# Two bias rows of a hybrid attention and gating layer: spread over the partitions by TensorE instead of loaded as equal rows

## The chip, the cores and the metric

The kernel runs on the 8 cores of one Trainium2 chip. Each core computes one of the 8 batch entries; the cores exchange nothing. The time of a run is the device time of the slowest core, in microseconds (us). Three runs of the kernel before took 498.07, 499.13 and 499.91 us; their median is 499.13 us.

## The reference, cut to what matters

For each batch entry, x is 4096 x 1024 in f32. The layer computes

```python
h = rmsnorm(x, norm_g)
proj = h @ w_in + b_in                      # 1024 -> 2816 columns
q, k, v, z_a, u_s, v_s, z_s = split(proj)   # 512,128,128,512,512,512,512
attn = banded_sink_attention(q, k, v, sinks) * silu(z_a)      # window 128, 8 heads of 64, 2 kv heads
u_s, v_s = gelu(u_s), gelu(v_s)
sgu = u_s * (W_s @ layernorm(v_s) + b_s) * silu(z_s)          # per chunk of 128 positions
out = rmsnorm(x + concat(attn, sgu) @ w_out + b_out, final_norm_g)
```

The change is about two slices of `b_in`: the 128 values added to `v` and the 512 values added to `v_s`, the gating input.

## The kernel before

**Tiling.** Each core walks 8 sections (`st`) of 512 positions, each of four tiles of 128 positions. In a section, the tiles of x are squared and summed, scaled by the reciprocal root (`square_x`, `rstd_x`, `scale_x`) and transposed to `xT` (`transpose_x`: by TensorE on an identity in sections 0 and 1, by DMA later). TensorE then multiplies by `w_all`, the bf16 input weights in 22 column blocks of 128 (`cb` 0 to 21: u 0-3, v_s 4-7, z_s 8-11, z_a 12-15, q 16-19, k 20, v 21). Most column blocks come out with channels on the partitions, where the bias is one value per partition and is read from `bias_fm`, columns 8 to 29 of the small constant `pack_a`. Two come out with positions on the partitions, so their bias varies along the free axis and has to stand in every partition: v (L637, reads `bv_bc`) and v_s (L668, reads `bvs`). Before, `bvs` is loaded from `bvs_bc`, 128 equal rows of 512 f32 (256 KB), and `bv_bc` is a slice of `pack_b`, 128 equal rows of 128 f32 (64 KB of the 198 KB).

**The opening.** x tiles 0 to 3 are issued first on the SP queue, `pack_a` on ACT's queue, then the 22 weight blocks of 512 KB each (`load_w`, L510-522). A weight block lands in one of 8 staging buffers (four in `xe`, four in `mixT`) and is scaled by `norm_g` and cast into `w_all` by DVE or POOL (L521); the load of block cb + 8 waits for that cast. In between stand the small constants, placed by `SMALL_AFTER` (L41): `bvs` behind block 2, `pb` behind 14, the gating weights and `bsB` behind 21. The four x tiles of section 1 are issued among blocks 14 to 18 (L38). TensorE runs 27 idle matmuls on zeros (L1000, `stir`) at the start and 4 more after each of the first three tiles' transposes; then u (`by_tile`, L575), v_s (`vs_first`, L647), and the other blocks (L588) as their weights come.

**What sets the order.** The program is a list of operations with estimated costs (`cost`, us) and priorities (`prio`). A planner (`Scheduler`) places them at build time, engine by engine, at the earliest estimated start, ties by priority; the result is a fixed instruction order on each engine with semaphore waits. Operations with a priority above -0.5 (`OPENING`) get a random shift from `SEEDS`, one seed per section, drawn by the operation's number in the list (L152-155). PSUM banks are handed out by the planner too: class "P" may hold 4 of the 8 at a time.

```python
    load_const(key, dst, src, eng="sp", kb=kb, prio=-1.4 + 0.01 * cb + 0.005, after=[w_op[cb]])   # L968
    o.prio += by if o.prio > OPENING and o.dsem is None else 0.0                                # L155
```

Of the kernel before, what the change touches and what calls it, by code (L numbers as in the profile page):

```python
# [8 lines left out]
F32 = mybir.dt.float32  # L9
# [15 lines left out]


PA_G, PA_BIAS, PA_ID, PA_W = 0, 8, 30, 94
PB_SINK, PB_LNB, PB_LNG, PB_BV, PB_MK, PB_MC, PB_W = 0, 4, 8, 12, 140, 332, 396


MIX0 = 5
# [6 lines left out]
X1_AFTER = (15, 16, 17, 18)  # L38
W_OUT_AFTER = 20
W_OUT_BEHIND = (2, 3, 3, 3, 3, 3, 3, 3)  # L40
SMALL_AFTER = {"bvs": 2, "pb": 14, "wT": 21, "bsB": 21}  # L41

STIR = (27, 4)
OPENING = -0.5
# [15 lines left out]
LAST_PARTS = (512, 384, 128)  # L60
LAST_APART = {NT - 4: "act", NT - 3: "dve", NT - 2: "dve"}

SEEDS = (49966, 300, 14147, 300, 300, 300, 300, 70794)
JITTER = 0.04


# [321 lines left out]
def build_program():  # L388
    nc = bass.Bass("TRN2", target_bir_lowering=False)

    def din(name, shape, dt=F32):
        return nc.dram_tensor(name, list(shape), dt, kind="ExternalInput").ap()
# [3 lines left out]
    wout_d = din("w_out", [D, D])  # L396
    pa_d = din("pack_a", [128, PA_W])
    pb_d = din("pack_b", [128, PB_W])
    bvs_d = din("bvs_bc", [128, 512])
    wT_d = din("sgu_wT", [128, 8, 128])  # L400
    bsB_d = din("bsB", [128, 4, 128])
    bout_d = din("bout_bc", [128, D])
# [3 lines left out]
    with ExitStack() as es:  # L406
        def sb(name, shape, dt):
            return es.enter_context(nc.sbuf_tensor(name, list(shape), dt))
# [21 lines left out]
        mixT = sb("mixT", [128, 2, 8, 512], BF16)  # L430
        sgt = sb("sgt", [128, 2, 512], F32)
        junk = sb("junk", [128, D], BF16)
        ones64 = sb("ones64", [128, 64], BF16)
        esink = sb("esink", [128, 4], F32)
        bvs = sb("bvs_sb", [128, 512], F32)
        WT = sb("WT_bf", [128, 8, 128], BF16)
# [4 lines left out]
        bias_fm = pa[:, PA_BIAS:PA_BIAS + NCB]  # L441
        ident = pa[:, PA_ID:PA_W].bitcast(BF16)
        lnb, lng = pb[:, PB_LNB:PB_LNB + 4], pb[:, PB_LNG:PB_LNG + 4]
        bv_bc = pb[:, PB_BV:PB_BV + 128]
        mask6, mask_c = pb[:, PB_MK:PB_MC].bitcast(BF16), pb[:, PB_MC:PB_W].bitcast(BF16)
        bout = sb("bout_sb", [128, D], F32)
        gf = sb("gf_sb", [128, D], F32)
# [15 lines left out]
        def bank(h):  # L463
            return pp[:, h.at, :]
# [155 lines left out]
        def qkv(st):  # L620
            qb, ks = st % 2, (st % 3) * 4
            v0 = st - 1.0
            for c in range(4):
                fm_group(st, CB_Q + c, qT[:, qb, c, :], ("qT", qb, c), None, v0 + 0.02 + 0.06 * c)
            fm_group(st, CB_K, kT[:, ks:ks + 4, :].rearrange("p a b -> p (a b)"), ("kT", st % 3), None, v0 + 0.26)
            h = Bank("P")
            xb = st % 2

            def mmv(e):
                for tt in range(4):  # L630
                    for k in range(8):
                        ins = e.matmul(bank(h)[:, tt * 128:(tt + 1) * 128], lhsT=xT[:, xb, k, tt * 128:(tt + 1) * 128],  # L632
                                       rhs=w_all[:, CB_V, k, :], start=(k == 0 and tt == 0), stop=(k == 7),
                                       skip_group_check=True)
                return ins
            G.op("pe", mmv, reads=[("xT", xb, t) for t in range(4)] + [("w", CB_V)], cost=1.79, alloc=[h], prio=v0 + 0.3, mode="full")
            G.op("dve", lambda e: e.tensor_tensor(out=v_r[:, ks:ks + 4, :], in0=bank(h).rearrange("p (a c) -> p a c", a=4),  # L637
                                                  in1=bv_bc.unsqueeze(1).to_broadcast([128, 4, 128]), op=ALU.add),
                 uses=[h], reads=["c_bv"], writes=[("v", st % 3)], cost=0.68, prio=v0 + 0.3)

        def vs_first(hs):
# [147 lines left out]
        def attention(st, j):  # L789
# [9 lines left out]
            def mmpv(e):  # L799
                def half(qh, what, g):  # L800
                    return pp[g * 64:(g + 1) * 64, hv.at + qh, what * 256:(what + 1) * 256]

                def weights(what, slot, r, g):
                    return ones64[r, :] if what else v_r[r, slot, g * 64:(g + 1) * 64]

                for what in range(1 if n else 2):
                    for kh, slot in ((0, cur), (1, prev)) if n else ((0, cur),):
                        r = slice(kh * 64, (kh + 1) * 64)
                        for g in range(2):
                            e.matmul(half(kh, what, g), lhsT=weights(what, slot, r, g), rhs=PT[r, p2, blk(BLK_Z[g])], start=what == 0,  # L810
                                     stop=False, skip_group_check=True)
                for what in range(2):
                    for qh, where, slot in ((1, BLK_X, cur), (0, BLK_Y, prev)) if n else ((1, BLK_X, cur),):
                        for g in range(2):
                            ins = e.matmul(half(qh, what, g), lhsT=weights(what, slot, slice(0, 128), g), rhs=(ET if what and n else PT)[:, p2, blk(where[g])],  # L815
                                           start=n == 0 and what == 0, stop=True, skip_group_check=True)
                return ins
# [127 lines left out]
        def finish_end(n, y, key, v0, parts):  # L945
# [15 lines left out]
            hold[NT - 2].after += (last_add[-1],)  # L961
            hold[NT - 3].after += (last_add[0],)

        def setup_late():
            stage_w = LR[:].rearrange("p a (h t) -> p (a h) t", t=128)
            def small(key, dst, src, name, kb):
                cb = SMALL_AFTER[name]
                load_const(key, dst, src, eng="sp", kb=kb, prio=-1.4 + 0.01 * cb + 0.005, after=[w_op[cb]])  # L968

            small("c_bvs", bvs[:], bvs_d, "bvs", 256)  # L970
            small(["c_sink", "c_lnb", "c_lng", "c_bv", "c_mask"], pb[:], pb_d, "pb", 198)
            small([("LR", 0), ("LR", 1)], stage_w, wT_d, "wT", 512)
            small("c_bsB", Cmat[:], bsB_d, "bsB", 256)
            G.op("dve", lambda e: e.tensor_tensor(out=WT[:], in0=stage_w, in1=mask_c.unsqueeze(1).to_broadcast([128, 8, 128]), op=ALU.mult),
                 reads=[("LR", 0), ("LR", 1), "c_mask"], writes=["WT"], cost=1.2, prio=-0.3, port=True)
            G.op("act", lambda e: e.activation(out=esink[:], in_=pb[:, PB_SINK:PB_SINK + 4], func=AF.Exp), reads=["c_sink"], writes=["esink"], cost=0.25,
                 prio=0, phase=PH_EXP)
            h = Bank("P")

            def cmat_mm(e):  # L980
                for jj in range(4):
                    for hh in range(2):
                        ins = e.matmul(bank(h)[hh * 64:(hh + 1) * 64, jj * 128:(jj + 1) * 128], lhsT=ones64[:, :], rhs=WT[:, 2 * jj + hh, :],
                                       start=(jj == 0), stop=True, skip_group_check=True)
                return ins
            G.op("pe", cmat_mm, reads=["ones64", "WT"], alloc=[h], cost=0.6, prio=-0.3, mode="col")

            def cm(e):
                for jj in range(4):
                    ins = e.scalar_tensor_tensor(out=Cmat[:, jj, :], in0=bank(h)[:, jj * 128:(jj + 1) * 128], scalar=lnb[:, jj:jj + 1],  # L990
                                                 in1=Cmat[:, jj, :], op0=ALU.mult, op1=ALU.add)
                return ins
            G.op("dve", cm, uses=[h], reads=["c_lnb"], writes=["c_bsB"] + [("Cmat", jj) for jj in range(4)], cost=1.3, prio=-0.3)
            load_const("c_bout", bout[:], bout_d, eng="sp", kb=512, prio=-0.3, after=[w_op[21]], reads=[("w_out", BOUT_AFTER)])
            load_const("c_gf", gf[:], gf_d, eng="sp", kb=512, prio=-0.3, after=[w_op[21]], reads=[("w_out", 7)])

        def stir(alloc, uses, count, after):
            def mm(e):
                for _ in range(count):
                    ins = e.matmul(bank(idle), lhsT=zsT[:, 0, 0:128], rhs=zsT[:, 0, :], start=True, stop=True)  # L1000
                return ins
            G.op("pe", mm, reads=[("zsT", 0)], alloc=alloc, uses=uses, cost=0.22 * count + (0 if uses else 4.0), prio=-9, mode="full", after=after)
# [15 lines left out]
        for tt in range(4):  # L1018
            square_x(0, tt)
            rstd_x(0, [tt])  # L1020
            scale_x(0, tt)
            o = transpose_x(0, tt)
            if tt < 3:
                stir((), [idle], STIR[1], [o])
        setup_late()
        gelu_part(0)
        silu_part(0)
# [39 lines left out]
def _host_layout(inp):  # L1067
# [10 lines left out]
    shared = {  # L1078
        "w_in": w_p,
        "w_out": w_out[rows, :],  # L1080
        "bvs_bc": np.broadcast_to(b_p[CB_VS:CB_VS + 4].reshape(1, 512), (128, 512)),
        "sgu_wT": np.asarray(inp["sgu_w"])[0].transpose(2, 0, 1),
        "bsB": np.repeat(np.asarray(inp["sgu_b"])[0].reshape(4, 2, 1, 128), 64, axis=2).reshape(4, 128, 128).transpose(1, 0, 2),
        "bout_bc": np.broadcast_to(np.asarray(inp["b_out"])[0], (128, D)),
# [3 lines left out]
    def words(m):  # L1088
        return np.ascontiguousarray(m.astype(ml_dtypes.bfloat16)).view(f32)
# [5 lines left out]
    lnb = np.asarray(inp["sgu_ln_b"])[0].reshape(4, 128).T  # L1095
    lng = np.asarray(inp["sgu_ln_g"])[0].reshape(4, 128).T
    shared["pack_a"] = np.concatenate([np.asarray(inp["norm_g"])[0].reshape(8, 128).T, b_p.T, words(eye)], axis=1)
    shared["pack_b"] = np.concatenate([sinks, lnb, lng, np.broadcast_to(b_p[CB_V], (128, 128)), words(mask6), words(mC)], axis=1)
    return {k: np.ascontiguousarray(v, dtype=f32) for k, v in shared.items()}


# [17 lines left out]
```

How the kernel before makes its waits and increments, by code:

```python
    def run(engine, items):  # L369
        for fn, waits, inc in items:
            for sem, val in waits:
                engine.wait_ge(sem, val)
            fn(engine).then_inc(inc[0], inc[1])
# [1 line left out]
    def sync(e):  # L375
        run(e, progs["sp"])
        for sem, val in finals.values():
            e.wait_ge(sem, val)
```

## Time and profile before

| what | value |
|---|---|
| three runs, median | 499.13 us (498.07 to 499.91) |
| profiled execution, its own time | 501.85 us |
| its span on the slowest core (core 5) | 500.3 us |
| spans of the eight cores | 495.9 to 500.3 us |
| busy on core 5 | PE 97%, DVE 71%, ACT 64%, POOL 36% |
| moved | 71.17 MB in the span, mean 142 GB/s |

The profiled execution took 501.85 us, 1.55 us more than the longest span of a core, and 2.72 us more than the median of the three runs. PE is TensorE's matmul row, PEld its weight loads, SPq the SP queue that issues transfers. An entry such as `L588` is a line of the kernel before. "Idle before" is the time an engine stood still just ahead of an instruction, and what ended it.

### The profile page before, as it was taken

The page shows a single profiled execution, that of the slowest core. Times are in us where ns is not written, and L with a number is a line of the kernel's source. Part 1 is how long each engine was busy: PE and PEld are TensorE (multiplying, and loading weights), DVE is VectorE, ACT ScalarE, POOL GpSimd, SP SyncE. Part 2 cuts the span into 40 slices and gives each one's busy share as a digit, 9 for nine tenths or more (in the row PEclk, how much of TensorE's full clock was granted, in tenths as well). Part 3 has the DMA queues.
Part 4 walks back from the last instruction along what each step waited for, and adds up shares of the span by engine and source line. Part 5 has one row for each costly group of instructions (what it writes and reads, how often), then busy time and mean ns, then how long its engine had stood idle before and what let it go on. Part 6 is the DMA issues. An engine that isn't in the chain of part 4 may idle for free.

```text
span 500.3 us, 10242 instructions; the slowest of 8 cores (495.9 to 500.3 us)
## 1 busy us (share of the span) xinstructions
PE 483.3 (97%) x3427; PEld 241.6 (48%) x3427; DVE 354.0 (71%) x537; ACT 319.8 (64%) x558; POOL 181.5 (36%) x223
## 2 busy tenths in 40 slices
PE   7797999999999999999999999999999999999994
PEld 3673455444544455444554445444554445444442
DVE  1678877596689448984696477773898547776795
ACT  3525665775688465965768565875659564567855
POOL 1114425444405121250245104470146733444144
PEclk9999899999999999999999999999999999999999
DMA  7999699488117911337413833355224422130035
GB/s 205 320 316 326 203 156 254 180 189 274 44 44 190 231 43 45 126 59 196 168 64 107 191 105 128 127 120 176 86 106 147 84 85 76 54 126 1 4 125 210
DMA packets 44116, 71.17 MB, mean 142 GB/s; under 512 B 27552, under 2 KB 27680, under 8 KB 44064
## 3 DMA queue, kind: packets, MB, share of 16 engines
q1 hardware_dynamic: 42768, 68.37, 44.9%
q0 software_dynamic: 1152, 2.10, 3.0%
q8 instruction: 28, 0.46, 0.4%
q14 instruction: 24, 0.20, 0.1%
q10 hardware_dynamic: 144, 0.05, 0.1%
HBM read 49.53 MB, written 16.78 MB: 133 GB/s over the span
## 4 chain that ended last, share of the span: by engine, by line
PE 82%; DMA 8%; DVE 4%; ACT 2%; issue 2%; SPq 0%; POOL 0%; DVEq 0%; ACTq 0%; POOLq 0%
PE pp L588 43%; PE pp L878 19%; PE pp L663 9%; DMA xe<-w_in 8%; PE pp L815 3%; PE pp L753 3%; PE pp L632 3%; PE pp L708 1%; PE pp L810 1%; DVE w_all L521 1%; ACT ET L771 1%; DVE ET L784 1%; ACT LR L835 0%; SPq L492 0%; DVE LR L841 0%
## 5 line engine op out<-in xcount | busy, mean ns | idle before, releaser
L588 PE MATMUL pp<-xT,w_all 128*128 128x512 bf16 x1056 | 237.0, 380 | 3.0 <-DVE w_all L521 2.7
L588 PEld LDWEIGHTS pp<-xT,w_all 128*128 128x128 bf16 x1056 | 101.6, 98 | 125.7 <-issue 7.2
L878 PE MATMUL pp<-w_out_bf,mixT 128*128 128x512 bf16 (+2 forms) x520 | 116.9, 376 | 0.4 <-DVE mixT L846 0.4
L869 POOL TENSOR_TENSOR xe<-xe,bout_sb 128x1024 f32<-128x1024 f32 x28 | 66.3, 2370 | 58.0 <-DMA xe<-x 20.6
L878 PEld LDWEIGHTS pp<-w_out_bf,mixT 128*128 128x128 bf16 x520 | 48.9, 98 | 58.3 <-issue 2.9
L771 ACT ACTIVATE ET<-pp 128x1536 bf16<-128x1536 f32 x32 | 46.4, 1451 | 12.4 <-PE pp L753 12.3
L663 PE MATMUL pp<-w_all,xT 128*128 128x512 bf16 x224 | 52.8, 384 | 0.6 <-DVE xe L885 0.3
L715 DVE SCALAR_TENSOR_TENSOR sgt<-pp,pack_b_sb,Cmat 128x512 f32<-128x512 f32 x32 | 23.7, 748 | 39.8 <-PE pp L708 39.1
L894 ACT ACTIVATE junk<-xe 128x1024 bf16<-128x1024 f32 x28 | 29.7, 1061 | 34.2 <-DVE xe L885 34.2
L899 POOL TENSOR_SCALAR st_fm<-st_fs 128x1 f32<-128x1 f32 x29 | 8.1, 281 | 111.6 <-ACT junk L894 110.9
L885 DVE TENSOR_TENSOR xe<-pp,xe 128x512 f32<-128x512 f32 x56 | 38.0, 685 | 8.6 <-PE pp L878 8.1
L835 ACT ACTIVATE LR<-pp,esink 128x128 f32<-128x128 f32 x128 | 36.4, 372 | 11.5 <-PE pp L815 7.6
L526 ACT ACTIVATE junk<-xa 128x1024 bf16<-128x1024 f32 x32 | 33.8, 1057 | 15.0 <-DMA xa<-x 14.3
L919 DVE SCALAR_TENSOR_TENSOR xe<-xe,st_fr,gf_sb 128x1024 f32<-128x1024 f32 x28 | 36.7, 1309 | 4.9 <-POOL st_fr L901 4.0
L670 ACT ACTIVATE vs_f<-vs_f 128x512 f32<-128x512 f32 x32 | 19.4, 625 | 27.0 <-DVE vs_f L668 23.8
L777 DVE TENSOR_TENSOR PT<-ET,pack_b_sb 128x1536 bf16<-128x1536 bf16 x32 | 32.3, 1010 | 5.6 <-ACT ET L771 4.9
L663 PEld LDWEIGHTS pp<-w_all,xT 128*128 128x128 bf16 x224 | 21.7, 99 | 27.6 <-issue 3.7
L616 ACT ACTIVATE zaT<-pp,pack_a_sb 128x512 bf16<-128x512 f32 x28 | 19.0, 686 | 23.7 <-PE pp L588 23.7
L485 ACT ACT_TABLE_LOAD x24 | 30.8, 1283 | 2.0 <-POOL ones L505 1.6
L784 DVE TENSOR_TENSOR ET<-PT 64x512 bf16<-64x512 bf16 x62 | 31.1, 503 | 1.3
L668 DVE TENSOR_TENSOR vs_f<-pp,bvs_sb 128x512 f32<-128x512 f32 x32 | 21.7, 685 | 13.2 <-PE pp L663 12.2
L841 DVE TENSOR_TENSOR LR<-LR,zaT 128x512 f32<-128x512 f32 x31 | 25.9, 834 | 6.7 <-ACT LR L839 6.5
(94 smaller groups left out, 583.2 us busy)
## 6 DMA issues: line engine op xcount, KB each, us to landing
xa<-x SPq DMA_DIRECT2D x32, 512.0 KB, 6.2
xe<-x SPq DMA_DIRECT2D x28, 512.0 KB, 3.4
out<-xe SPq DMA_DIRECT2D x28, 512.0 KB, 2.7
xe<-w_in SPq DMA_DIRECT2D x12, 512.0 KB, 14.0
mixT<-w_in SPq DMA_DIRECT2D x10, 512.0 KB, 15.6
w_out_bf<-w_out POOLq DMA_DIRECT2D x8, 256.0 KB, 11.9
out<-w_all SPq DMA_DIRECT2D x3, 512.0 KB, 2.7
LR<-sgu_wT SPq DMA_DIRECT2D x1, 512.0 KB, 20.7
```

What stands on the lines that cost most here:

```text
L485: return lambda e: e.activation(out=dmy[:, 1:2], in_=dmy[:, 0:1], func=func)
L526: G.op("act", lambda e: e.activation(out=junk[:], in_=xa[:, tt, :], func=AF.Square, accum_out=st_ss[:, par, tt:tt + 1]), reads=[("xa", tt) ...
L588: ins = e.matmul(bank(h), lhsT=w_all[:, cb, k, :], rhs=xT[:, xb, k, :], start=(k == 0), stop=(k == 7))
L663: ins = e.matmul(bank(h), lhsT=xT[:, xb, k, tt * 128:(tt + 1) * 128], rhs=w_all[:, CB_VS:CB_VS + 4, k, :], start=(k == 0), stop=(k == 7))
L771: G.op("act", lambda e: e.activation(out=ET[:, p2, :].rearrange("p (g b) -> p g b", g=2), in_=raw(), func=AF.Exp, scale=0.125), uses=[h], ...
L777: return e.tensor_tensor(out=v, in0=raw, in1=m, op=ALU.mult)
L784: return e.tensor_tensor(out=at[:, pick], in0=z[:, pick], in1=z[:, rest], op=ALU.add)
L835: ins = e.activation(out=LR[:, lb, c * 128:(c + 1) * 128].rearrange("p (h q) -> p h q", h=2), in_=banks_of(hv)[:, :, 256 + c * 64:256 + (c ...
L869: G.op("pool", lambda e: e.tensor_tensor(out=buf[:, s, :], in0=buf[:, s, :], in1=bout[:], op=ALU.add), reads=["c_bout"], writes=[key], cos ...
L878: ins = e.matmul(bank(h)[:, 0:width], lhsT=mixT[:, mb, ec, tt * 128:(tt + 1) * 128], rhs=w_out[:, ec, cols], start=(ec == 0), stop=(ec == 7))
L885: G.op("dve", lambda e, cols=cols, h=h, width=width: e.tensor_tensor(out=buf[:, s, cols], in0=bank(h)[:, 0:width], in1=buf[:, s, cols], op ...
L919: G.op("dve", lambda e: e.scalar_tensor_tensor(out=src, in0=src, scalar=st_fr[:, s:s + 1], in1=gf[:], op0=ALU.mult, op1=ALU.mult), reads=[ ...
```

## The change

The 256 KB transfer of `bvs_bc` is gone, and `pack_b` is 128 columns narrower (198 to 134 KB). In their place `spread_biases` makes the rows on the core. `bias_fm` (128 channels by 22 blocks, one value per partition) is split into three bf16 parts on DVE; each part's column is multiplied by the identity, which gives diagonal matrices; TensorE multiplies them by a 128 x 128 matrix of ones, which puts the sum of the three diagonals into every partition; ACT copies the two results from PSUM. `ones64` grows from 64 to 128 columns; its other users take the first 64. The diagonals lie in `ET`, which attention first uses much later. The list of operations is ten longer behind this point, and three of the eight seeds are others.

```diff
-PB_SINK, PB_LNB, PB_LNG, PB_BV, PB_MK, PB_MC, PB_W = 0, 4, 8, 12, 140, 332, 396
+PB_SINK, PB_LNB, PB_LNG, PB_MK, PB_MC, PB_W = 0, 4, 8, 12, 204, 268
-SMALL_AFTER = {"bvs": 2, "pb": 14, "wT": 21, "bsB": 21}
+SMALL_AFTER = {"pb": 14, "wT": 21, "bsB": 21}
-SEEDS = (49966, 300, 14147, 300, 300, 300, 300, 70794)
+SEEDS = (17612, 300, 30261, 300, 300, 300, 300, 61515)
...
-        ones64 = sb("ones64", [128, 64], BF16)
+        ones64 = sb("ones64", [128, 128], BF16)
...
-        bv_bc = pb[:, PB_BV:PB_BV + 128]
+        bv_bc = sb("bv_bc", [128, 128], F32)
+        b_part = sb("b_part", [128, 3, NCB], BF16)
+        b_left = sb("b_left", [128, NCB], F32)
...
+        def spread_biases():
+            parts = ET[:].rearrange("p a b -> p (a b)")[:, 0:1920]
+            d_vs = parts[:, 0:1536].rearrange("p (i c t) -> p i c t", i=3, c=4)
+            d_v = parts[:, 1536:1920].rearrange("p (i t) -> p i t", i=3)
+            for i in range(3):
+                left = b_left[:] if i else bias_fm
+                G.op("dve", lambda e, i=i, left=left: e.tensor_copy(out=b_part[:, i, :], in_=left), reads=["b_left"] if i else ["c_biasfm"],
+                     writes=[("b_part", i)], cost=0.1, prio=-8)
+                if i < 2:
+                    G.op("dve", lambda e, i=i, left=left: e.tensor_tensor(out=b_left[:], in0=left, in1=b_part[:, i, :], op=ALU.subtract),
+                         reads=["c_biasfm", ("b_part", i)], writes=["b_left"], cost=0.1, prio=-8)
+            at = [("b_part", i) for i in range(3)] + ["c_ident"]
+            G.op("dve", lambda e: e.tensor_tensor(out=d_vs, in0=ident.unsqueeze(1).unsqueeze(1).to_broadcast([128, 3, 4, 128]),
+                                                  in1=b_part[:, :, CB_VS:CB_VS + 4].unsqueeze(3).to_broadcast([128, 3, 4, 128]), op=ALU.mult),
+                 reads=at, writes=[("ET", 0), ("ET", 1)], cost=1.7, prio=-8)
+            G.op("dve", lambda e: e.tensor_tensor(out=d_v, in0=ident.unsqueeze(1).to_broadcast([128, 3, 128]),
+                                                  in1=b_part[:, :, CB_V:CB_V + 1].to_broadcast([128, 3, 128]), op=ALU.mult),
+                 reads=at, writes=[("ET", 0), ("ET", 1)], cost=0.5, prio=-8)
+            for key, d, dst, cost in (("c_bvs", d_vs, bvs, 0.66), ("c_bv", d_v, bv_bc, 0.17)):
+                h = Bank("P")
+                width = dst.shape[1]
+
+                def mm(e, h=h, d=d, width=width):
+                    for i in range(3):
+                        ins = e.matmul(bank(h)[:, 0:width], lhsT=ones64[:], rhs=d[:, i], start=(i == 0), stop=(i == 2))
+                    return ins
+                G.op("pe", mm, reads=["ones64", ("ET", 0), ("ET", 1)], alloc=[h], cost=cost, prio=-2.95, mode="full")
+                G.op("act", lambda e, h=h, dst=dst, width=width: e.activation(out=dst[:], in_=bank(h)[:, 0:width], func=AF.Copy), uses=[h],
+                     writes=[key], cost=0.2 + 0.45 * width / 512, prio=-1.9)
...
-            small("c_bvs", bvs[:], bvs_d, "bvs", 256)
-            small(["c_sink", "c_lnb", "c_lng", "c_bv", "c_mask"], pb[:], pb_d, "pb", 198)
+            small(["c_sink", "c_lnb", "c_lng", "c_mask"], pb[:], pb_d, "pb", 134)
...
+        spread_biases()
         setup_late()
```

## Rows read from the trace of the kernel before

**Rows 1.** The eight cores: span and mean granted clock.
```profile
core 0: 495.9 us, clock 0.996
core 3: 499.3 us, clock 0.996
core 4: 495.9 us, clock 0.997
core 5: 500.3 us, clock 0.995
```
**Rows 2.** Busy time by stretch (PE, PEld, DVE, ACT, POOL, clock, DMA): core 5, last core 3.
```profile
20.00:50.00 30.00, 27.52 (x306) 19.41 (x302) 23.13 (x31) 11.55 (x19) 7.98 (x12) 1.00 0.99 325
45.00:50.00 5.00, 2.52 (x17) 1.17 (x16) 3.92 (x8) 4.22 (x9) 1.03 (x3) 1.00 0.99 332
50.00:55.00 5.00, 4.73 (x15) 1.82 (x16) 3.94 (x8) 4.87 (x8) 1.65 (x3) 0.66 1.00 321
300.00:400.00 100.00, 100.00 (x664) 49.20 (x662) 72.95 (x112) 67.81 (x116) 45.14 (x50) 1.00 0.41 122
...
50.00:55.00 5.00, 5.00 (x30) 2.50 (x29) 4.68 (x7) 4.97 (x8) 2.23 (x4) 1.00 1.03 282
```
**Rows 3.** Core 5, chain that ended last, to 75 us: start, us, what.
```profile
31.32 17.38 DMA xe<-w_in
...
48.79 1.24 DVE w_all L521
50.02 0.24 issue
50.27 2.63 PE pp L588 x8
52.90 2.67 PE pp L663 x8
55.57 0.45 PE pp L559 x8
56.01 1.73 PE pp L588 x8
```
**Rows 4.** PE's waits to 75 us: core 5, core 3, core 0; total, times, longest.
```profile
PE pp L588 <- DVE w_all L521: 2.7, 2, 2.1
...
PE pp L588 <- DVE w_all L521: 2.5, 2, 1.5
...
PE pp L588 <- ACT zsT L616: 0.8, 1, 0.8
```
**Rows 5.** DMA issues of the whole span: KB each, median us to landing.
```profile
xe<-w_in SPq DMA_DIRECT2D x12, 512.0 KB, 14.0
bvs_sb<-bvs_bc SPq DMA_DIRECT2D x1, 256.0 KB, 13.8
...
out<-w_all SPq DMA_DIRECT2D x1, 256.0 KB, 2.5
...
pack_b_sb<-pack_b SPq DMA_DIRECT2D x1, 198.0 KB, 12.0
pack_a_sb<-pack_a ACTq DMA_DIRECT2D x1, 47.0 KB, 4.9
```
**Rows 6.** Core 5, timeline to 60 us: start, us, instruction, idle before.
```profile
1.06 0.40 ACTq L481 DMA_DIRECT2D pack_a_sb<-pack_a  x1
...
1.88 8.45 PE L1000 MATMUL pp<-zsT 128*128 128x512 bf16 x27 [1.88 <-DVE zsT L1016]
...
8.53 0.19 POOL L532 TENSOR_SCALAR st_ms<-st_ss 128x1 f32<-128x1 f32 x1 [7.20 <-ACT junk L526]
...
9.52 0.75 DVE L541 TENSOR_SCALAR xn<-xa,st_rs 128x1024 bf16<-128x1024 f32 x1 [7.79 <-POOL st_rs L535]
...
10.53 0.61 PE L559 MATMUL pp<-pack_a_sb,xn 128*128 128x128 bf16 x8 [0.21 <-DVE xn L541]
...
14.67 1.10 POOL L532 TENSOR_SCALAR st_ms<-st_ss 128x1 f32<-128x1 f32 x1 [0.48 <-ACT junk L526]
...
18.55 7.31 PE L575 MATMUL pp<-xT,w_all 128*128 128x128 bf16 x128
...
45.74 1.89 PE L588 MATMUL pp<-xT,w_all 128*128 128x512 bf16 x8 [0.65 <-DVE w_all L521]
...
46.82 1.83 ACT L616 ACTIVATE zsT<-pp,pack_a_sb 128x512 bf16<-128x512 f32 x3
```
**Rows 7.** Costs: small and wide operations like those added.
```profile
L674 DVE BATCH_NORM_AGGREGATE st_mv<-st_bn 128x2 f32<-128x6 f32 x4 | 0.7, 176 | 0.0
L521 DVE TENSOR_TENSOR w_all<-xe,pack_a_sb 128x1024 bf16<-128x1024 f32 x4 | 4.9, 1222 | 1.4 <-DMA xe<-w_in 1.3
L616 ACT ACTIVATE zsT<-pp,pack_a_sb 128x512 bf16<-128x512 f32 x4 | 2.5, 680 | 0.0
...
L777 DVE TENSOR_TENSOR PT<-ET,pack_b_sb x32: 942/957/2101, 69.1 to 475.0; 128x1536 bf16<-128x1536 bf16 x32
```
**Rows 8.** PE's waits from 72 us on, core 3: total, times, longest.
```profile
PE pp L588 <- DMA xT<-xn: 1.2, 1, 1.2
```

More of the change, by code:

```diff
@@ L398, in build_program @@
     pb_d = din("pack_b", [128, PB_W])
-    bvs_d = din("bvs_bc", [128, 512])
     wT_d = din("sgu_wT", [128, 8, 128])
@@ L637, in qkv @@
             G.op("dve", lambda e: e.tensor_tensor(out=v_r[:, ks:ks + 4, :], in0=bank(h).rearrange("p (a c) -> p a c", a=4),
-                                                  in1=bv_bc.unsqueeze(1).to_broadcast([128, 4, 128]), op=ALU.add),
+                                                  in1=bv_bc[:].unsqueeze(1).to_broadcast([128, 4, 128]), op=ALU.add),
                  uses=[h], reads=["c_bv"], writes=[("v", st % 3)], cost=0.68, prio=v0 + 0.3)
@@ L803, in weights @@
                 def weights(what, slot, r, g):
-                    return ones64[r, :] if what else v_r[r, slot, g * 64:(g + 1) * 64]
+                    return ones64[r, 0:64] if what else v_r[r, slot, g * 64:(g + 1) * 64]
                 for what in range(1 if n else 2):
@@ L982, in cmat_mm @@
                     for hh in range(2):
-                        ins = e.matmul(bank(h)[hh * 64:(hh + 1) * 64, jj * 128:(jj + 1) * 128], lhsT=ones64[:, :], rhs=WT[:, 2 * jj + hh, :],
+                        ins = e.matmul(bank(h)[hh * 64:(hh + 1) * 64, jj * 128:(jj + 1) * 128], lhsT=ones64[:, 0:64], rhs=WT[:, 2 * jj + hh, :],
                                        start=(jj == 0), stop=True, skip_group_check=True)
@@ L1080, in _host_layout @@
         "w_out": w_out[rows, :],
-        "bvs_bc": np.broadcast_to(b_p[CB_VS:CB_VS + 4].reshape(1, 512), (128, 512)),
         "sgu_wT": np.asarray(inp["sgu_w"])[0].transpose(2, 0, 1),
@@ L1097, in _host_layout @@
     shared["pack_a"] = np.concatenate([np.asarray(inp["norm_g"])[0].reshape(8, 128).T, b_p.T, words(eye)], axis=1)
-    shared["pack_b"] = np.concatenate([sinks, lnb, lng, np.broadcast_to(b_p[CB_V], (128, 128)), words(mask6), words(mC)], axis=1)
+    shared["pack_b"] = np.concatenate([sinks, lnb, lng, words(mask6), words(mC)], axis=1)
     return {k: np.ascontiguousarray(v, dtype=f32) for k, v in shared.items()}
```

## The prediction

> **What bounds the kernel now.** I read the spans of the eight cores first: they end between 495.9 and 500.3 us, and core 5 is the last [rows 1]. On core 5 the table of busy time by stretch then shows two kernels in one. From about 75 us on PE is full, 100.00 of 100 us in the stretch shown, so nothing there can be shortened by taking work off another engine, and whatever PE loses or wins earlier goes straight to the end. Between 20 and 50 us the DMA engines are full instead, 0.99 busy at 325 GB/s [rows 2]. The chain of waits says what that means: up to 50 us it runs through the loading of weight blocks, the last link being a block issued at 31.32 us that took 17.38 us to land, its cast, and then PE without a break [rows 3]. PE's waits give the amount: 2.7 us in two waits for cast weights on core 5 (0.65 us at 45.74 and 2.1 us ahead of the matmuls at 50.27), 2.5 us on core 3; core 0 waits 0.8 us there, but for ACT's silu copies [rows 4, 6]. On core 5 the granted clock is 0.66 between 50 and 55 us and 1.00 before: after the gap PE runs at the lower of its levels (1.2 against 2.4 GHz). The two groups of eight matmuls that follow take 2.63 and 2.67 us where the same eight take 1.73 us a little later [rows 2, 3]; that is 0.90 + 0.94 = 1.84 us.
>
> **Bytes removed.** 512 x 128 x 4 bytes of bvs and 128 x 128 x 4 bytes of pack_b are 262 + 66 = 328 KB (thousands of bytes). Both stand in the queue ahead of the weight block that releases PE at 50.27 (block 16; bvs follows block 2, pack_b block 14). A block takes 14.0 us to land [rows 5] while 512 KB at 325 GB/s would take 1.6, so some eight are always queued and the engines never run dry: time there is bytes by rate. 328 KB / 325 GB/s = 1.01 us, of which bvs is 0.81. The two removed sources land long before they are read, so nothing else is gained from them. SP also issues one transfer less; its cost is hidden by the same queue. Bounds of the term: 0, if what PE waits for next is as late, and 1.8 us, if the half-size bvs costs the 1.6 of a weight block. I take 1.01. What is late next on core 5 is ACT's silu copies, which end at 46.82 + 1.83 = 48.65 us [rows 6]; PE waits until 50.27, so 1.01 us can be taken out before they bind. On core 0 they bind already [rows 4], so it gains little, but it ends 4.4 us ahead of core 5 [rows 1].
>
> A transfer of 256 KB that goes out alone, the last store of the kernel, takes 2.5 us [rows 5], three times bvs's share of the bytes. The page DMA: Bandwidth & Descriptors of the Trainium skill, section Anatomy of one DMA, says why: 2.0 us fixed and then 436 GB/s; by its figures the two removed sources would be an estimated 0.75 us of bytes, or 2.75 us with bvs's fixed part in series. The trace speaks against the series: blocks keep the engines 0.99 busy while each is 14 us in flight [rows 2, 5].
>
> **DVE added.** Five operations on 128 x 22, each waiting for the one before. The nearest row is the tiny aggregate at 0.176 us [rows 7]; a hand-over from DVE to PE takes 0.24 us [rows 3], one within DVE between nothing and that. So each is 0.18 to 0.42; I take 0.3, the middle, 1.5 us for five (0.9 to 2.1). The two multiplications write 1536 and 384 elements. The row with 1536 elements takes 0.957 us, but its second operand is repeated along an outer axis; L521, whose second operand is repeated along the inner axis as here, takes 1.222 us for 1024 [rows 7]. I take the latter's rate: 1.83 + 0.46 = 2.3 us (bound below: 0.96 + 0.24 = 1.2). The sum is 3.8 us, between 2.1 and 4.4. pack_a is issued at 1.06 and lands 4.9 us later, at 6.0 [rows 5, 6], so DVE is done at 9.8 us, between 8.1 and 10.4. On core 5 DVE is idle until 9.52, when the first tile's scaling starts [rows 6]: the new work fits, or delays it by 0.3 us, 0.9 at most. PE is held by the idle matmuls until 1.88 + 8.45 = 10.33 us anyway. Tile 0's transposes start at 10.53, and tile 1 follows it on DVE; a delay of 0.3 to 0.9 us is what reaches them. Take the cover away (an x tile that lands before pack_a's work is done, PE without idle matmuls) and the price is the whole 3.8 us.
>
> POOL is beside it: L532 of one tile takes 1.10 us on core 5 at 14.67, while DVE casts a block, against 0.19 us for the same line at 8.53 [rows 6]. By that row the new multiplications can hold the first tile's root by 0.9 us. The page SBUF — State Buffer of the Trainium skill, section Who interferes with whom, speaks against this change here: a DVE instruction with two SBUF inputs and a GpSimd one that reads SBUF exclude each other for the whole instruction, so by it the hold could be the longer multiplication's whole 1.83 us. The row agrees: L532 there ends with the cast of 1.22 us. The hold falls on the first tile alone, under the same idle matmuls; it enters rival (b).
>
> **PE and ACT added.** Three matmuls of 512 columns at 1.73 / 8 = 0.216 us and three of 128 columns at 7.31 / 128 = 0.057 us [rows 3, 6]: 0.82 us, placed about the first tiles' transposes where PE stands idle or stirs. ACT copies 512 and 128 columns: 0.68 us by L616 [rows 7], and at most that again, 1.0 together as I take it (0.7 to 1.4). They stand in ACT's queue among squares and scalings of x between 10 and 17 us, so a tile may come up to 1 us later. PE starts u at 18.55 on core 5 [rows 6], runs into the weights' limit at 45 and then has 2.7 us to spare, 1.7 after the gain. I cost this at nothing; without the cover it is 1.0 + 0.8 us. v_s and v read their new rows after 30 us, so nobody waits for them.
>
> **Order redrawn.** Ten more operations and three new seeds give every shifted operation another draw, so the static order of all eight sections changes. PE's full stretch bounds what that can win (nothing to speak of before the tail). What it can lose is seen where PE does wait: core 3 loses 1.2 us once to a late transposing DMA [rows 8]. I take 0.
>
> **Sum.** Against the profiled execution: core 5 loses 1.01 us, and 1.84 more if its clock holds; it would end at 497.5, and core 3, 499.3 - 1.01 = 498.3, would be last. With the 1.55 us around the span that is 499.85 where it had 501.85. The median of the runs is already 2.72 us under that execution, less than core 3 alone would give (499.3 + 1.55), so its waits are smaller than those I can see; I carry over only the bytes: 499.13 - 1.01 = **498.1 us**.
>
> **The rivals.**
> (a) *Clock and bytes.* The shorter wait keeps the clock up too, in the usual run as well: 499.13 - 1.01 - 1.84 = 496.3. For it: core 3, with 2.5 us of such waits of at most 1.5, shows 1.00 in the same 5 us [rows 2, 4]; against it: the median may not contain the fall at all, and 1.7 us of waiting remain. Chance 0.18.
> (b) *Hidden.* In the usual run PE waits for ACT's silu copies, as core 0 does, or the copies and the multiplications eat the gain in the x path: 499.1. Chance 0.20.
> (c) *Slower: the redrawn order.* It puts PE behind DMA transposes in the full stretch. Each such wait costs 1.2 us; from one on the gain is gone, two give 499.13 - 1.01 + 2.4 = 500.5, and three, 501.7, would be measured as slower. For it: core 3 shows one already; against it: on core 5 PE has none there. Chance 0.14, half of it with three or more.
> (d) *A transfer saved in series.* If bvs held the queue for the 2.5 us of a lone transfer of its size [rows 5], its removal and the 0.2 us of pack_b give 499.13 - 2.7 = 496.4. Against it: the DMA row has no gap to save. Chance 0.02. The fixed 2.0 us of the Trainium skill's page DMA: Bandwidth & Descriptors would be the mechanism.
> The forecast itself keeps 0.46.
>
> **How the numbers follow.** A measurement of this kernel tells about 0.5%, 2.5 us, from no change. Faster than that (under 496.6) are (a) and (d), less a fifth of (a), which clears that line by 0.3 us only, and with a twentieth of the forecast with the byte term at its upper bound: 0.18. Slower (over 501.6) is the half of (c): 0.07. The rest, 0.75, is within. The range takes in (a) with the byte term at its upper bound, 499.13 - 1.84 - 1.8 = 495.5, and two waits of (c), 500.5; what lies outside is half of (c) and little else, which allows for what I have not thought of.
>
> **What would show it.** Right: the DMA row stays at 0.99 to 50 us and block 16's cast starts about 1 us earlier than 48.79; PE's waits on L521 fall from 2.7 to about 1.7 us on core 5; the added DVE work ends before 9.8 us and u starts at 18.5 or before; from 75 us on PE is full as before. Wrong: u starting over 1 us later, PE waiting for ACT's or DVE's new instructions, the weight blocks landing no earlier, or new waits after 75 us.

## The result, and the profile after

The change made the kernel slower: 503.29 us (median of 6 runs, 501.81 to 503.44) against 498.76 us (6 runs of the kernel before). The ratio is 1.0071 with a 95% interval of 1.0046 to 1.0096, so about 3.5 us (2.3 to 4.8) are lost where I forecast 1 us won. (The two medians lie 4.5 us apart; everything below is compared by ratios.) The profiled execution of the changed kernel took 503.22 us, like the median; its last core is core 7. Below, a ratio is turned into microseconds at 498.6 us.

Spans of the cores (us, mean granted clock), as [rows 1]:

```profile
core 0: 500.9 us, clock 0.992
...
core 3: 500.3 us, clock 0.996
...
core 5: 498.1 us, clock 0.996
...
core 7: 501.6 us, clock 0.994
```

Four of the eight cores end above 500 us, where one did before, although the profiled execution of before was itself 3.1 us above the median of its 6 runs: what is lost isn't lost on one core.

Busy time by stretch on core 7 (PE, PEld, DVE, ACT, POOL, clock, DMA share, GB/s), the stretches of [rows 2]:

```profile
20.00:50.00 30.00, 27.04 (x295) 18.81 (x292) 24.43 (x30) 9.62 (x16) 5.80 (x10) 1.00 1.01 336
45.00:50.00 5.00, 3.86 (x18) 1.50 (x16) 4.77 (x7) 2.74 (x5) 4.31 (x7) 1.00 1.00 320
50.00:55.00 5.00, 4.90 (x34) 2.70 (x35) 4.78 (x9) 5.00 (x9) 2.77 (x6) 1.00 0.91 315
300.00:400.00 100.00, 98.93 (x661) 48.27 (x656) 74.48 (x112) 71.51 (x123) 40.80 (x46) 1.00 0.40 117
```

The DMA engines are as full as before up to 50 us. The stretch from 300 to 400 us, which I had called full at 100.00 of 100, now has a hole of 1.07 us, far from anything the change touches.

PE's waits on core 7, first up to 75 us, then behind it (total, times, longest), as [rows 4, 8]:

```profile
PE pp L560 <- DVE xn L542: 2.3, 1, 2.3
...
PE pp L576 <- issue: 1.8, 1, 1.8
PE pp L589 <- ACT zsT L617: 1.2, 1, 1.2
...
PE pp L589 <- ACT zsT L617: 0.8, 2, 0.4
PE pp L589 <- DVE vs_f L669: 0.7, 1, 0.7
```

(Lines have moved by one: L589 is L588 of before, L542 is L541, and so on.) The wait for cast weights, 2.7 us on core 5 before, is gone (whether the change took it away is asked below, at spread_added). PE now waits 1.2 us for ACT's first silu; all eight cores have this wait between 45 and 50 us, 1.0 to 1.7 us long. Three more waits of this family stand behind 75 us; the earlier one is for DVE's scaled first x tile.

DMA issues (KB each, us to landing), as [rows 5]:

```profile
xe<-w_in SPq DMA_DIRECT2D x12, 512.0 KB, 12.0
...
pack_b_sb<-pack_b SPq DMA_DIRECT2D x1, 134.0 KB, 11.0
```

A weight block lands in 12.0 us, not 14.0. That alone doesn't show the removed bytes at work: in spread_added, below, where they are all still there, it is 12.4.

Timeline of core 7 (start, us, instruction, idle before), the lines that answer to [rows 6]:

```profile
6.08 0.18 DVE L971 CAST b_part<-pack_a_sb 128x22 bf16<-128x22 f32 x1 [4.35 <-DMA pack_a_sb<-pack_a]
6.36 0.18 DVE L974 TENSOR_TENSOR b_left<-pack_a_sb,b_part 128x22 f32<-128x22 f32 x1
...
7.50 1.76 DVE L977 TENSOR_TENSOR ET<-pack_a_sb,b_part 128x1536 bf16<-128x1536 bf16 x1
...
8.07 1.24 POOL L533 TENSOR_SCALAR st_ms<-st_ss 128x1 f32<-128x1 f32 x1 [6.71 <-ACT junk L527]
...
9.37 0.56 DVE L980 TENSOR_TENSOR ET<-pack_a_sb,b_part 128x384 bf16<-128x384 bf16 x1
9.46 0.88 POOL L536 TENSOR_TENSOR st_rs<-st_ms,neghalf 128x1 f32<-128x1 f32 x1
...
10.44 0.75 DVE L542 TENSOR_SCALAR xn<-xa,st_rs 128x1024 bf16<-128x1024 f32 x1 [0.52 <-POOL st_rs L536]
...
11.45 1.01 PE L560 MATMUL pp<-pack_a_sb,xn 128*128 128x128 bf16 x8 [2.30 <-DVE xn L542]
...
13.96 1.38 PE L989 MATMUL pp<-ET,ones 128*128 128x512 bf16 x6
...
15.27 0.60 ACT L992 ACTIVATE bvs_sb<-pp 128x512 f32<-128x512 f32 x1
...
17.97 0.61 PE L576 MATMUL pp<-xT,w_all 128*128 128x128 bf16 x8
...
35.49 1.89 DVE L669 TENSOR_TENSOR vs_f<-pp,bvs_sb 128x512 f32<-128x512 f32 x3 [3.57 <-PE pp L648]
...
46.15 0.68 DVE L669 TENSOR_TENSOR vs_f<-pp,bvs_sb 128x512 f32<-128x512 f32 x1
```

This view shows both suspects. At 7.5 to 9.9 us stands the new work: GpSimd's L533 takes 1.24 us beside the long multiplication (0.19 in [rows 6]), L536 0.88, the first tile is scaled at 10.44, and PE is dry for 2.30 us. At 35 to 46 us nothing is new, yet the order is another one. On this core five weight casts (L522) now stand between the first three additions of the gating bias and the fourth, and the fourth starts 10.66 us behind the first. Before, it was four casts, with a fifth on GpSimd, and 42.15 - 33.19 = 8.96 us on core 5. ACT's gelu of that row, its table load and the silu for which PE waits all stand behind the fourth addition.

So there were two theories. **The work**: the spread itself (the hold of the first tile, ACT's copies, PE's six matmuls) costs 3 to 4.5 us. **The order**: the list of operations, ten longer, and the new seeds shift the planner's draws for everything, and the order that it then writes costs it.

### The profile page after: what moved, and what is told of

The parts are those of the page before. It is cut to its first block, busy times and chain, and to the rows that moved or that the text cites. A ratio compares the mean times of both kernels' runs of the same rounds, so it can differ in the third digit from the quotient of the medians.

```text
span 501.6 us, 10255 instructions; the slowest of 8 cores (498.1 to 501.6 us)
## 1 busy us (share of the span) xinstructions
PE 484.0 (97%) x3433; PEld 241.8 (48%) x3433; DVE 363.4 (72%) x543; ACT 325.9 (65%) x565; POOL 179.8 (36%) x219
## 4 chain that ended last, share of the span: by engine, by line
PE 80%; DVE 5%; issue 5%; ACT 4%; DMA 3%; POOL 1%; DVEq 0%; ACTq 0%; POOLq 0%; SPq 0%
PE pp L589 40%; PE pp L879 20%; PE pp L664 8%; PE pp L816 3%; PE pp L754 3%; PE pp L633 3%; DMA mixT<-w_in 2%; DVE w_all L522 2%; PE pp L709 1%; DMA xa<-x 1%; PE pp L811 1%; DVE xe L886 1%; ACT junk L527 1%; PE pp L560 1%; DVE xn L542 1%
## 5 line engine op out<-in xcount | busy, mean ns | idle before, releaser
L589 PE MATMUL pp<-xT,w_all 128*128 128x512 bf16 x1056 | 236.3, 379 | 2.8 <-ACT zsT L617 2.0
L589 PEld LDWEIGHTS pp<-xT,w_all 128*128 128x128 bf16 x1056 | 101.3, 98 | 127.3 <-issue 8.2
L785 DVE TENSOR_TENSOR ET<-PT 64x512 bf16<-64x512 bf16 x62 | 34.6, 559 | 1.6
L617 ACT ACTIVATE uT<-pp,pack_a_sb 128x512 bf16<-128x512 f32 x32 | 21.7, 680 | 14.0 <-PE pp L576 12.3
```

What stands on the lines that cost most here:

```text
L589: ins = e.matmul(bank(h), lhsT=w_all[:, cb, k, :], rhs=xT[:, xb, k, :], start=(k == 0), stop=(k == 7))
L617: G.op("act", lambda e: e.activation(out=dst, in_=bank(h), func=func, bias=bias), uses=[h], reads=["c_biasfm"] + ([("u0", cb, tt) for tt i ...
L785: return e.tensor_tensor(out=at[:, pick], in0=z[:, pick], in1=z[:, rest], op=ALU.add)
```

## The experiments

The planner adds a random draw (JITTER 0.04) to each operation's priority, and counts the bytes of the loads. To change one thing at a time I gave each operation that both kernels have the draw that it has in the kernel before (a counter that the spread doesn't advance), and let the planner go on counting the removed bytes where the text says "order of before". The traces show the engines' instructions then in the order of before, but for the instructions that are named and, where the spread is in, two small moves in the opening: one copy to xT goes from ACT to VectorE, and eight of u's matmuls go ahead of eight others.

**First batch: work against order.** The edits:

```
loads_gone         the loads removed, no spread, rows set to zero; order of before
spread_added       the loads kept, the spread added into two unread buffers; order of before
spread_old_order   the whole change; order of before
after_shrunk       kernel after; of the spread's instructions each is left, but shrunk:
-  d = ident * b_part            (1536 and 384 columns)
+  b_left[:, 10] = bias_fm[:, 0] (one column)
-  3 matmuls of 512 (128) columns, copy of 512 (128) columns
+  1 matmul of 128 columns, copy of one column; rows set to zero
```

In loads_gone and after_shrunk the two biases are left out of the result.

> Both removed sources gone, nothing in their place: the two rows of biases are filled with zeros by GpSimd at the start, so the biases of v and of the gating input are left out. The planner still counts the removed bytes and draws as before, so the order on every engine is that of the kernel before. This prices the bytes alone. My forecast's term: 1.01 us less than before, about 497.8. If ACT's silu copies hold PE wherever the weight blocks come earlier (rival b): no difference, 498.8.

> The kernel before with all its loads and its order, plus the whole spreading work into rows that nobody reads. This prices the work alone. Theory of the work (DVE's diagonals stand ahead of the first tile's scaling, hold GpSimd's root, PE runs dry and drops its clock on some cores): 3 to 4.5 us over before, 502 to 503. Theory of the order (the redrawn order of the whole kernel costs it): at most the 0.8 us of the six matmuls, 498.8 to 499.6.

> The whole change (loads gone, rows spread by TensorE), but in the order of the kernel before with the spreading work put in: the planner draws as before and still counts the removed bytes. Theory of the work: spread_added less what loads_gone wins, so 501 to 503. Theory of the order: at or under before, 497.8 to 499.

> The kernel after, its order and its loads unchanged, but each instruction of the spreading work shrunk to one element or one small matmul, and the two rows filled with zeros by GpSimd at the start; the biases of v and of the gating input are left out. This prices the new order alone. Theory of the work: back to before or under it, 497.8 to 499.5. Theory of the order: it stays at the time of after less a few tenths, 502.5 to 503.3.

Measured against the runs of before on the same chip (498.61 us):

```
loads_gone         ratio 0.9992 [0.9981, 1.0004]   -0.4 us
spread_added       ratio 1.0012 [1.0001, 1.0023]   +0.6 us
spread_old_order   ratio 1.0015 [1.0005, 1.0025]   +0.7 us
after_shrunk       ratio 1.0080 [1.0066, 1.0095]   +4.0 us
```

The theory of the work falls. The spread whole costs 0.6 us in the order of before, and taking nearly all of it out of the changed kernel gives nothing back: 4.0 us are lost without it, 3.5 with it, and the intervals overlap. The order is what costs. The removed bytes are worth 0.4 us (between a loss of 0.2 and a gain of 0.9). Why not 1.0? First PE's waits between 40 and 60 us in loads_gone, core 5:

```profile
PE pp L596 <- ACT zsT L624: 0.6, 1, 0.6
```

On six cores PE waits for ACT's silu, 0.6 to 1.1 us, and on two for weights, 0.9 and 1.2 us. Now the same window in spread_added, which still loads every byte, on core 1 (its last) and core 0, and the landing of its weight blocks on core 1:

```profile
PE pp L595 <- ACT zsT L623: 0.7, 1, 0.7
```
```profile
PE pp L595 <- DVE w_all L528: 1.0, 1, 1.0
```
```profile
xe<-w_in SPq DMA_DIRECT2D x12, 512.0 KB, 12.4
```

The picture is nearly the same with the bytes in: six cores wait 0.7 us for the silu, one waits 1.0 us for weights, one for neither. before_new_draws, below, loads every byte too and has no spread: there one core waits for weights between 40 and 60 us, for 0.2 us. So, as far as these traces tell, the 2.7 us and the 14.0 us belong to the one profiled execution of before (501.85 us; this one, 499.68, is near the median of its kernel, 499.5). Elsewhere the silu is late already, and there was little for the bytes to win.

**Second batch: which part of the order, and is it these draws?** Two kernels have the whole change, with the draws of after for one part and those of before for the other; the part "opening" is the planner's section 0 (set-up, the first 512 positions and the projections of the next 512). The planner counts the true bytes in early_redrawn and those of before in late_redrawn. (`draws` come from the seeds of before, `draws_a` from those of after; `o.d` is the counter.) One has the whole change with the draws of before, but the planner sees the true bytes. One is the kernel before with the draws of after.

```
-  by = JITTER * draws[o.section][o.n]
+  by = JITTER * (draws_a[o.section][o.n] if o.section == 0 else draws[o.section][o.d])   early_redrawn
+  by = JITTER * (draws_a[o.section][o.n] if o.section else draws[o.section][o.d])        late_redrawn
+  by = JITTER * draws[o.section][o.d]                                                    change_old_draws
-  SEEDS = (49966, 300, 14147, 300, 300, 300, 300, 70794)
+  SEEDS = (17612, 300, 30261, 300, 300, 300, 300, 61515)      before_new_draws
+  G.m += 10    (the counter skips the place of the spread)       before_new_draws
```

> The whole change; the planner's draws are those of after in section 0 (set-up and first tile) with the true bytes, and those of before in all later sections (the plan still differs there where the opening hands on another state). Theory of the opening (most of the order's 3.5 us between 499.8 and 503.3 are lost before 100 us, at the silu of the first tile and the weight casts): 502 to 503.5 us. Theory of the later sections (the opening costs 0.8 us, PE's lag between 200 and 400 us the rest): 500.2 to 501 us, with PE's wait for the silu at 45 to 50 us as in after (1.0 us or more) and its lag between 200 and 400 us as in the kernel before.

> The whole change; the opening is planned with the draws and bytes of before, all later sections with the draws of after. Theory of the opening: 499.5 to 500.3 us, as with the whole order of before (499.8). Theory of the later sections: 502 to 503 us, with PE falling behind by 2 to 3 us more than in the order of before between 200 and 400 us.

> The whole change with the draws of before for every operation that both kernels have; the planner sees the true bytes, so the order is still another one than before's. If the new draws themselves are the bad ones: 499.3 to 500.3 us. If the order of before is one good draw out of many and any other costs some us: 501 to 504 us.

> The kernel before, with its loads and no spread, planned with the draws of after. Nothing of the change is in it but the redraw. Theory of the order (the redraw costs about 4 us whatever is loaded or spread): 501 to 504 us. If the redraw costs only together with the change's own work: 498 to 499.5 us.

Measured (before: 498.36 us on this chip):

```
early_redrawn      ratio 1.0066 [1.0054, 1.0078]   +3.3 us
late_redrawn       ratio 1.0035 [1.0023, 1.0048]   +1.7 us
change_old_draws   ratio 1.0151 [1.0133, 1.0168]   +7.5 us
before_new_draws   ratio 1.0300 [1.0282, 1.0319]  +15.0 us
```

Against spread_old_order (ratio 1.0015) the opening, draws and bytes together, costs 0.51%, 2.5 us, and the later sections 0.20%, 1.0 us. Together that is 3.5 us where the whole costs 0.56%, 2.8 us: the same within the intervals. So I had the larger share of the theory of the opening right, and neither theory whole. Part of what the later sections cost can be read from PE's busy time from 200 to 400 us (PE, clock, DMA share, GB/s), core 7, in spread_old_order, early_redrawn, late_redrawn and after, in this order:

```profile
200.00:400.00 200.00, 199.38 (x1298) 1.00 0.43 123
```
```profile
200.00:400.00 200.00, 199.59 (x1324) 1.00 0.42 123
```
```profile
200.00:400.00 200.00, 198.51 (x1318) 1.00 0.42 121
```
```profile
200.00:400.00 200.00, 198.46 (x1316) 1.00 0.42 123
```

PE is idle for 1.5 us with the late draws of after, and for 0.4 to 0.6 us with those of before, whatever the opening. The waits behind it are the three of the family above: in late_redrawn, as in after, 0.8 us for zsT in two and 0.7 us for vs_f in one. The late draws give some of it back behind 400 us: from 400 to 460 us PE is busy for 59.98 us in late_redrawn and 59.66 in spread_old_order. So the idle time between 200 and 400 us shows where the loss begins, and isn't its net size.

The last two runs are the strongest. In before_new_draws the kernel before, with its loads and without a trace of the spread, loses 15 us by new draws alone. PE's waits on its last core, core 6, from 40 us to the end:

```profile
PE pp L881 <- DVE mixT L849: 9.8, 4, 3.7
PE pp L881 <- DMA w_out_bf<-w_out: 1.6, 1, 1.6
```

The output product (out tiles) stands on PE ahead of other work while its operand is not ready: four waits of up to 3.7 us, two of them before 100 us (5.4 us) and two behind 460 (4.5 us), where with the old draws the last core waits for the same producer once, for 0.4 us. change_old_draws differs from spread_old_order only in the loads that the planner counts; there it is another wait again, 2.3 us at L757 for DVE's vs_f on core 0. Three redrawn orders thus cost 3.5, 7.5 and 15 us, each at other places. All are slower than the order of before; whether its seeds had been picked for that, no run here shows.

**Third batch: is the opening's loss the late silu?** In the kernel after I exchanged two neighbours in VectorE's list, so that the fourth addition goes ahead of one weight cast; in spread_old_order I made the opposite move (there the cast also passes the normalization behind the addition). And in the order of before I made the spread without the multiplications.

```
   order = sched.run()
+  dve = order["dve"]; dve[39], dve[40] = dve[40], dve[39]        cast_behind (kernel after)
+  dve = order["dve"]; dve.insert(38, dve.pop(40))                cast_ahead (order of before)

-  d = ident * b_part (two multiplications); matmul(lhsT=ones, rhs=d)                spread_columns
+  matmul(lhsT=b_part[:, i, c:c + 1].to_broadcast([128, 128]), rhs=ident), 15 times
```

> The kernel after the change with one exchange in VectorE's list: the fourth addition of the gating input's bias goes ahead of the weight cast that stands before it (1.1 us). If VectorE's casts ahead of that addition make the first silu late: the addition starts 1.1 us sooner, PE's wait for the silu at 45 to 50 us falls from 1.2 to 0.3 us or less, and the time is about 1 us under after's (502.1 to 502.7 us). If that wait is made good later, or the matmuls then wait for the cast instead: 503.0 to 503.6 us.

> The whole change in the order of before, with the opposite move: one weight cast is taken from behind the fourth addition to ahead of it. If the first silu's lateness is a loss for good: PE's wait for it grows from 0.5 by about 1.1 us, and the time is 500.4 to 501.0 us. If it is made good later: 499.5 to 500.1 us, as without the move (499.8).

> The whole change in the order of before, with the spread made another way: the bias columns themselves, repeated along the free axis, are the stationary operand and the identity moves (15 matmuls of 128 columns), so the two multiplications on VectorE (1.76 and 0.56 us, and GpSimd held beside them) are gone; the five small operations and ScalarE's two copies stay. If the multiplications are what the spread costs: 498.6 to 499.2 us. If the copies or the matmuls cost it: 499.5 to 499.9 us, as with the multiplications.

Measured (before: 500.79 us on this chip; so ratios, not times, are to be compared with those above):

```
cast_behind        ratio 1.0078 [1.0054, 1.0102]   (after: 1.0071)
cast_ahead         ratio 1.0021 [1.0007, 1.0034]   (spread_old_order: 1.0015)
spread_columns     ratio 1.0005 [0.9991, 1.0020]   (spread_old_order: 1.0015)
```

Neither move changes the time beyond the intervals. If that one addition were the opening's 2.5 us, cast_behind would have won them back; its interval and that of after leave room for a gain of 1.4 us at most. A gain or loss of the 1.1 us that one cast takes they don't exclude, so there the waits have to tell. PE's waits between 40 and 60 us in cast_behind, core 7:

```profile
PE pp L589 <- DVE w_all L522: 1.1, 3, 0.5
```

The wait of 1.2 us for the silu is gone, and 1.1 us of waits for weight casts have come instead. (On the other cores they are 0.3 to 1.0 us, and two of them still wait 0.4 us for the silu.) In cast_ahead the wait for the silu didn't grow as I had expected: PE waits 0.7 to 1.4 us for weight casts instead, on every core. VectorE is the engine that both wait for: 4.77 of 5 us busy from 45 to 50 us in the changed kernel. What is taken ahead there puts back something else. My theory that one cast ahead of one addition is what costs the opening 2.5 us falls. The late silu is one place where the loss shows; PE's wait for it between 40 and 60 us, core 7, in spread_old_order and in early_redrawn:

```profile
PE pp L592 <- ACT zsT L620: 0.5, 1, 0.5
```
```profile
PE pp L594 <- ACT zsT L622: 1.2, 1, 1.2
```

Over the eight cores it is 0.3 to 0.7 us in the first and 1.0 to 1.2 us in the second, so it holds some 0.7 of the 2.5 us. Where the rest goes, and which of the moved instructions cause it, stays open.

The spread by columns does what it should. On core 4 of spread_columns, the timeline shows GpSimd unhindered, and 15 matmuls in 1.00 us:

```profile
8.83 0.19 POOL L536 TENSOR_SCALAR st_ms<-st_ss 128x1 f32<-128x1 f32 x1 [7.45 <-ACT junk L530]
9.17 0.55 POOL L539 TENSOR_TENSOR st_rs<-st_ms,neghalf 128x1 f32<-128x1 f32 x1
...
12.14 1.00 PE L983 MATMUL pp<-pack_a_sb,b_part 128*128 128x128 bf16 x15
```

Its ratio is 0.10% (0.5 us) below that of the spread with multiplications, but the intervals overlap, and it isn't faster than the kernel before. No version here beat the kernel before by more than its interval; the most that is to be had, loads_gone without any spread, is 0.4 us.

## Why the prediction was wrong

**The step that failed** is "Order redrawn": "PE's full stretch bounds what that can win ... What it can lose is seen where PE does wait: core 3 loses 1.2 us once ... I take 0." The trace of before shows the waits of one order. It cannot show those of another, so it was no bound on the loss. The runs put 2.8 us of the 3.5 there (1.0071 against 1.0015 in the order of before; by the two intervals 1.4 to 4.1 us), and 4.0 with the spread shrunk; two other redraws cost 7.5 and 15 us. PE's 100.00 of 100 us from 300 to 400 us [rows 2] was a property of that order too: with the new one it is 98.93.

**Rival (c)** had the right cause and sign, with a chance of 0.14. Its mechanism was too narrow. I let the redraw cost only by the one kind of late wait I had seen, DMA transposes at 1.2 us each [rows 8]. None shows among the waits of any core of the changed kernel. The longer waits that do show are for ACT's silu, in the opening and later, and for DVE's vs_f in the later sections. The opening as a whole costs 2.5 us and the later sections 1.0 us; the waits that I can name account for only a part of the first.

**Bytes removed.** The term was mis-sized: 0.4 us (at most 0.9) for 1.01. The DMA engines do stay full up to 50 us, as I said. But the wait that the bytes were to shorten, 2.7 us for cast weights, I had read from one execution, 2.72 us above the median that I knew. In spread_added, with every load in place, PE waits for a weight cast on one core of eight (1.0 us) and for ACT's silu on six (0.7 us). I had named the silu copies as what is late next, with 1.01 us to go before they bind; in spread_added they bind already. That is the first half of rival (b).

**DVE added** was right. The five small operations start 0.28 us apart (0.3 taken), the multiplications take 1.76 and 0.56 us (1.83 and 0.46), and all is done at 9.93 us, 3.85 after the start (3.8).

**POOL** was sized a little low by the term that I took. L533 is held by 1.24 - 0.19 = 1.05 us where I took 0.9, and L536 by another 0.33, which I didn't count. L533 ends at 9.31 us, with the long multiplication (7.50 + 1.76 = 9.26). The trace so agrees with the rule of the Trainium skill, page SBUF — State Buffer, section Who interferes with whom, that the pair exclude each other for the whole instruction.

**The cover** was thinner than I said. On core 7 the idle matmuls end 2.30 us ahead of the first transposes, not at 10.33 us. The granted clock is 0.83 between 10 and 20 us, so for part of it PE is at the lower of its levels: the eight transposes take 1.01 us where the next eight take 0.61. Yet this costs little. u starts at 17.97 us there (18.55 on core 5 before), and the spread in the order of before, hold and all, costs 0.6 us. Most of PE's wait of 2.3 us is thus not in the time.

**PE and ACT added.** PE's six matmuls take 1.38 us for 0.82, ACT's copies 0.60 + 0.27 = 0.87 for 1.0. Costed at nothing, they are within the 0.6.

**The clock** (rival (a)): from 50 to 55 us core 7 is granted 1.00, so the fall to 0.66 that core 5 had before isn't there. Nor is it in spread_added, which keeps the loads: all eight cores are granted 1.00 there from 50 to 55 us. In before, too, it stands on core 5 alone. **The transfer in series** (rival (d)) is excluded by loads_gone: 2.7 us aren't there. (The section that I cited for it, Anatomy of one DMA on the Trainium skill's page DMA: Bandwidth & Descriptors, gives its figures for transfers issued by GpSimd; bvs and pack_b were issued on the SP queue.)

Taken together: bytes and spread, measured in one kernel, +0.7 (-0.4 and +0.6 when measured apart, the same within the intervals), and +2.8 for the order make the 3.5.

## What to carry to other kernels

Where a planner writes the order and breaks near ties by random draws, any edit of the list of operations is two changes: its own work and a redraw of the rest. The trace of before bounds the first, not the second; to price the edit, hold the order (same draw for the same operation, same bytes for the planner) and measure each by itself. And a wait that is to be shortened has to be there in a usual execution: the trace of before, 3.1 us above the median, showed 2.7 us of waiting for weights, and removing the bytes was worth 0.4 of the 1.0 us that I took from it.

## What the runs showed that I had not expected

A redraw with nothing else changed cost the kernel before 3.0% (15 us); I had taken it for noise about zero. The GpSimd operation behind the held one is long too (L536, 0.88 for 0.55 us, while the short multiplication runs). A stationary operand can be one column repeated 128 times along its free axis: 15 such matmuls of 128 columns took 1.00 us, and their weight loads 1.04 us beside them, against 1.76 + 0.56 us on VectorE for building the diagonal blocks. An exchange of two neighbours in one engine's list, which took away a wait of 1.2 us, changed the time by nothing that the runs can tell.
